# Gate rows through a scratch row in memory in place of TensorE transposes, in a two-layer decoder trunk

## What is computed

```python
for layer in range(DEPTH):
    mod = cond @ ada_w[layer] + ada_b[layer]
    sh1, sc1, g1, sh2, sc2, g2 = jnp.split(mod[:, None, :], N_MOD, axis=-1)
    h = rms_norm(x) * (1.0 + sc1) + sh1
    # layer 0: even_mixer (attention A and B), layer 1: odd_mixer (attention C)
    x = x + g1 * y
    h = rms_norm(x) * (1.0 + sc2) + sh2
    x = x + g2 * swiglu(h, ffn_w_in[layer], ffn_w_out[layer])
return rms_norm(x, final_norm)
```

## Time and profile before

| | |
|---|---|
| median of 3 runs | 2246.99 us (2246.51 to 2250.19) |
| profiled execution | 2246.95 us, of it the span 2245.2 us |
| PE busy | 2155.9 us (96%) |
| weight loads of PE (PEld) busy | 1783.2 us (79%) |
| DVE busy | 1622.7 us (72%) |
| ACT busy | 973.1 us (43%) |
| DMA | 594.08 MB, mean 265 GB/s |

### The profile page before, as it was taken

How to read it: one execution, slowest core, us unless ns; L and a number is a source line. 1 busy time by engine, 2 the same in 40 slices (tenths; PEclk the granted TensorE clock), 3 DMA queues, 4 the chain that set the end, 5 groups by cost and what they waited for, 6 DMA issues and landing times.

```text
span 2245.2 us, 26214 instructions
## 1 busy us (share of the span) xinstructions
PE 2155.9 (96%) x9996; PEld 1783.2 (79%) x9996; DVE 1622.7 (72%) x1696; ACT 973.1 (43%) x1276; POOL 10.0 (0%) x22
## 2 busy tenths in 40 slices
PE   3789999989999999999999999989999999999998
PEld 2578887878888888888887888878888888888886
DVE  5988898987789988777667666586665554555446
ACT  4344444454443344434445444454443344433444
POOL 0000000000000000000000000000000000000000
PEclk9899999999999999999999999999999999999999
DMA  9977878859889999977755533357765555555543
GB/s 389 421 290 311 330 300 356 329 230 372 325 325 353 385 381 378 383 284 288 283 213 230 197 127 117 122 189 300 283 249 202 199 188 187 187 190 196 193 152 150
DMA packets 82446, 594.08 MB, mean 265 GB/s; under 512 B 9296, under 2 KB 9328, under 8 KB 10672
## 3 DMA queue, kind: packets, MB, share of 16 engines
q1 hardware_dynamic: 81072, 588.29, 68.2%
q0 software_dynamic: 1280, 4.51, 0.7%
HBM read 590.66 MB, written 2.10 MB: 264 GB/s over the span
## 4 chain that ended last, share of the span: by engine, by line
PE 83%; DVE 10%; DMA 3%; ACT 2%; DVEq 1%; issue 0%; SPq 0%; ACTq 0%
PE ps L1344 25%; PE ps L1346 25%; PE ps L1345 25%; DVE w_lo L800 3%; PE ps L1332 2%; DVE ada_raw L804 2%; DMA gate<-in_ada 2%; DMA raw<-in_ffn_out 1%; PE ps L1439 1%; DVE gate L804 1%; PE ps L1372 1%; ACT w_hi L478 1%; PE ps L1374 1%; PE ps L1373 1%; DVE xT_lo L919 0%; PE ps L1438 0%
## 5 line engine op out<-in xcount | busy, mean ns | idle before, releaser
L800 DVE TENSOR_TENSOR w_lo<-raw,w_hi 128x1024 fp32r<-128x1024 f32 x728 | 880.5, 1222 | 470.3 <-ACT w_hi L478 466.1
L478 ACT ACTIVATE w_hi<-raw 128x1024 fp32r<-128x1024 f32 x728 | 763.0, 1060 | 987.3 <-PE ps L1346 801.6
L1344 PE MATMUL ps<-w_hi,xT_hi 128*128 128x512 f32 x1940 | 769.4, 397 | 31.8 <-DVE xT_lo L1057 24.3
L1346 PE MATMUL ps<-w_hi,xT_lo 128*128 128x512 f32 x1940 | 760.3, 392 | 0.0
L1345 PE MATMUL ps<-w_lo,xT_hi 128*128 128x512 f32 x1940 | 759.5, 392 | 0.0
L1344 PEld LDWEIGHTS ps<-w_hi,xT_hi 128*128 128x128 f32 x1940 | 367.3, 189 | 112.6 <-DVE xT_lo L1057 26.6
L1346 PEld LDWEIGHTS ps<-w_hi,xT_lo 128*128 128x128 f32 x1940 | 366.7, 189 | 78.0
L1345 PEld LDWEIGHTS ps<-w_lo,xT_hi 128*128 128x128 f32 x1940 | 367.5, 189 | 74.2
L804 DVE SCALAR_TENSOR_TENSOR ada_raw<-ada_raw,cond 128x2048 f32<-128x2048 f32 x176 | 401.8, 2283 | 16.8 <-DMA ada_raw<-in_ada 15.7
L1344 PE MATMUL ps<-w_hi,hT_hi 128*128 128x512 f32 x896 | 352.6, 393 | 2.7 <-DVE work L1243 1.1
L1346 PE MATMUL ps<-w_hi,hT_lo 128*128 128x512 f32 x896 | 349.5, 390 | 0.0
(11 more groups left out here) (178 smaller groups left out, 952.7 us busy)
## 6 DMA issues: line engine op xcount, KB each, us to landing
ada_raw<-in_ada SPq DMA_DIRECT2D x176, 1024.0 KB, 6.6
raw<-in_ffn_in SPq DMA_DIRECT2D x176, 1024.0 KB, 4.9
raw<-in_ffn_out SPq DMA_DIRECT2D x88, 1024.0 KB, 5.2
raw<-in_ab_in SPq DMA_DIRECT2D x48, 1024.0 KB, 8.3
raw<-in_swa_in SPq DMA_DIRECT2D x20, 1024.0 KB, 4.8
raw<-in_ab_out SPq DMA_DIRECT2D x16, 1024.0 KB, 7.3
raw<-in_swa_out SPq DMA_DIRECT2D x16, 1024.0 KB, 4.8
spare<-in_ada SPq DMA_DIRECT2D x8, 1024.0 KB, 8.2
```

The lines of the kernel that those rows point to most:

```text
L478: nc.scalar.activation(w_hi[:, p % PAIRS, :, :], raw[:, t % RAW, 2 * (p % 2):2 * (p % 2) + 2, :], ACT.Copy).then_inc(hi_ready, 1)
L800: tt(w_lo[:, p % PAIRS, :, :], raw[:, (p // 2) % RAW, 2 * (p % 2):2 * (p % 2) + 2, :], w_hi[:, p % PAIRS, :, :].bitcast(F32), ALU.subtract ...
L1344: mm(out, hi[:, kt, tok], w_hi[:, q % PAIRS, k, :], start=(kt == 2 * ps0), stop=False)
L1346: last = mm(out, lo[:, kt, tok], w_hi[:, q % PAIRS, k, :], start=False, stop=(kt == 2 * ps1 - 1))
```

## The change

GpSimd makes the gate rows. For each of the four gates it waits for `mods_ready`, writes the vector from `mod` to a scratch row in memory (`gate_rows`, new), waits until that has landed, and loads the row back, broadcast to all partitions, into `gate`. The loads wait for what frees the tile: `o_done` 4 or 12, or the `evacuated` count at the end of the projection before. DVE only waits for the landing; PE's transposes and its waits for the copy go. The order in GpSimd's queue is as in the diff: the write of the third row stands ahead of the first C bias, the third load behind the last bias of C_OUT, the fourth row ahead of `final_norm`.

```diff
+    rows = nc.dram_tensor("gate_rows", (4, D), F32, kind="Internal").ap()
...
-        gate_spread = sem("gate_spread")
-        gate_copied = sem("gate_copied")
+        row_written = sem("gate_row_written")
+        row_landed = sem("gate_row_landed")
...
+            def gate_row(n, vec):
+
+                pool.wait_ge(mods_ready, GATES_AT[n])
+                pool.dma_start(rows[n].rearrange("(k p) -> p k", p=P), mod[:, vec // 6, vec % 6, :], allow_slow_non_contiguous=True).then_inc(row_written, 16)
+                pool.wait_ge(row_written, 16 * (n + 1))
+
+            def load_row(n):
+                pool.dma_start(gate[:, :], rows[n].partition_broadcast(P)).then_inc(row_landed, 16)
+
+            gate_row(0, G1[0])
+            pool.wait_ge(o_done, 4)
+            load_row(0)
+            gate_row(1, G2[0])
+            pool.wait_ge(evacuated, EVAC_CREDIT + FFN[0][0][0].block0)
+            load_row(1)
+            gate_row(2, G1[1])
             for c in range(5):
...
+            pool.wait_ge(o_done, 12)
+            load_row(2)
+            pool.wait_ge(evacuated, EVAC_CREDIT + FFN[1][0][0].block0)
+            gate_row(3, G2[1])
+            load_row(3)
             pool.wait_ge(evacuated, EVAC_CREDIT + FFN[1][0][1].block0)
...
             def gate_row(n):
 
-                dve.wait_ge(gate_spread, n + 1)
-                nc.vector.tensor_copy(gate[:, :], bank(4, 4)).then_inc(gate_copied, 1)
-                dve.drain()
+                dve.wait_ge(row_landed, 16 * (n + 1))
...
-            def spread_gate(n, vec):
-
-                pe.wait_ge(mods_ready, GATES_AT[n])
-                for c in range(KT):
-                    last = tr(ps[:, 4 * 512 + c * P:4 * 512 + (c + 1) * P],
-                              mod[:, vec // 6, vec % 6, c:c + 1].broadcast_to([P, P]))
-                last.then_inc(gate_spread, 1)
-
...
-                if n == 12:
-                    spread_gate(0, G1[0])
-                if n == 14:
-                    pe.wait_ge(gate_copied, 1)
...
-                            if s == 0 and p == fout.pairs - 1:
-                                spread_gate(1 + 2 * layer, G2[layer])
...
-                    pe.wait_ge(gate_copied, 2 + 2 * layer)
...
-                if n == 16:
-                    spread_gate(2, G1[1])
...
-            pe.wait_ge(gate_copied, 3)
```

## The result

| | before | changed |
|---|---|---|
| median | 2246.99 us | 2256.02 us (2254.27 to 2258.07, 5 runs) |
| ratio to before | | 1.0040, 95% interval 1.0029 to 1.0051 |
| span of the profiled execution | 2245.2 us | 2253.8 us |

The changed kernel is slower by 0.4%, about 9 us. The forecast was 2242.8 us, with a range of 2238.5 to 2264 us.

What follows compares the result with a forecast made beforehand. TensorE was taken to bound the kernel (83% of the chain), with VectorE or the weight supply on it at two gate rows; -2.37 + 1.6 - 1.75 - 1.75 = -4.2 us gave 2242.8 us, range 2238.5 to 2264.

Steps and rivals of the forecast that it cites:

- Place 0, the gain: First gate row, copy ending at 424.16 us: VectorE's removed copy sets the gain, 2.37 us, not 1.75 + 2.37.
- Place 0, the write: Write of the first row at 306 to 316 us: charged nothing, up to W kept for the range.
- W: How long a row's write keeps the DMA engines from the weights: taken as 4 us, between 0 and 26.
- The row that was set aside, sinks: Transfer of 128 pieces of 128 bytes, all reading the same bytes; in proportion 26 us a write, not taken.
- the estimate of 1.3 us for W: From the skill page's 10.5 ns a packet, 128 packets; would put the sum 2.7 us lower.
- Place 1: Second gate row, copy at 687.19 us, chain through the weight supply: -2.37 + 4 = +1.6 us.
- Place 2: Third gate row, copy at 1455.25 us, TensorE bound: removing 16 transposes gains 1.75 us.
- Place 3: Fourth gate row, copy at 1708.38 us, TensorE bound: gain 1.75 us; row may land as late as 1712.9.
- rival (b): Row comes late through GpSimd's serial steps though W is small: 2244 to 2250 us, chance 0.17.
- Is the row in time at place 1?: Second row lands at 687.7 us; VectorE may stand until 689.6 before the chain is later than before.
- Rival (c): Small pieces hold the engines as beside sinks; no gain from W = 8.2, 2265 to 2281 us at 26; chance 0.23.
- The general form 2247 - 8.2 + W: Whole kernel's time for any W, as long as the second row isn't later than 689.6 us.

Runs made afterwards that it cites:

- the sorted row: Kernel before with rows 0, 1, 3 (then only 0, 3) written in 64-byte pieces, loaded into spare, put in feature order by ScalarE: ratios 0.9993 and 0.9990.
- writes only: Kernel before, transposes and copies kept, plus the four writes in 4-byte pieces, whose rows nobody reads: 2259.06 us, ratio 1.0049.
- place 0 alone: Kernel before with only the first gate row through memory, in 4-byte pieces, the others made as before: 2251.39 us, ratio 1.0015.
- the other execution: The changed kernel, unaltered, run and profiled again on another occasion, against the kernel before: 2255.11 against 2247.64 us, ratio 1.0038.

## Why the prediction was wrong, step by step

**Place 0, the gain.** Forecast 2.37 us; measured 2.4 in each of the four profiles in which that row was moved as in the change, 2.2 with the sorted row. DVE did set it, not the sum of both engines. Right.

**Place 0, the write (charged with 0).** This step failed. Its reason was that PE has no gap at 306 and DMA is less than half used soon after the earlier trace rows. The write cost 3.8 and 6.6 us in the two profiles of the change, 4.4 with writes only, some 5.8 by the ratio of place 0 alone. The two loads behind the write landed 7.8 and 7.7 us late, the stock ran out, and the slack that follows came too late for it; written at 332, with half of the hole in time without a load, it still cost 5.8. Where it cost most, a part is PE at its lower clock behind its stand, a term that the prediction didn't have. The text kept "up to W" for the range, so the doubt was there, but the sum took the end that was cheapest.

**W.** Taken as 4 us, between 0 and 26; measured 8.4 us at place 1. (That is against 410 GB/s. In the same stretch of the kernel before 0.6 us of it are missing too.) The mechanism of the step, engines that serve pieces and weights in turn, puts half of the feeding time on the weights. GpSimd's part in the feeding is 1.17 us (a price in proportion to the 128 rows of a broadcast load was 8.6), so the base of the estimate was wrong, and so was the half: while the pieces go, the weights get next to nothing. The row that was set aside, sinks with 34 to 164 GB/s, had the right form, one address or few; only its price per piece, 26 us / 128 = 200 ns, was too high. 8.4 us over 128 pieces an engine is 66 ns. The objection to it was that these pieces go to different addresses. So they do, but to neighbouring ones, and with 4 bytes in each 256 the hole became a dip. (In rows 6 six slices lie between 34 and 164 GB/s, not seven, and nine with the return, not ten, lack the 670 KB; the 26 us stand.)
On the page "DMA: Bandwidth & Descriptors" of the Trainium skill, the section "Rules for kernel authors" has a strided last dimension as one descriptor per element and wants it contiguous. The runs agree: some 13 us to landing against 5.3. Its section "Specifications" has an engine reading, modifying and writing below 512 bytes; that alone doesn't order these runs, since pieces of 64 bytes and pieces of 4 bytes 256 bytes apart are below it too and cost nothing that the medians show. By the estimate of 1.3 us for W from the section "Bandwidth" the sum would have been further off still; 8.4 is six times that.

**Place 1.** Forecast -2.37 + W. With W = 8.4 this is +6.0; measured +5.8 in both, or +6.3 and +6.1 up to pair 240. Right in that a hole at this place goes to the end, and mis-sized in W. That the sum comes out to 0.2 us is in part luck: it has no term for the clock, and 1.7 of the 5.8 us are PE at its lower level behind its second stand (the step at that pair is 1.6 us in both executions). Without it 4.1 us are left of the 6.0, so the delay of the supply didn't arrive in full; where the rest was made up, nothing here shows.

**Place 2.** Forecast -1.75, measured 0 (0.0 in both executions of the change, ratio 0.9999 alone). This step failed too. It took "PE bound" for granted and didn't ask what is next in PE's stream behind the transposes. It is a wait for DVE's half of an output block, which the transposes had covered.

**Place 3.** Forecast -1.75; measured -1.8 alone and -1.4 and -1.1 in the change. The row was late, as rival (b) had it. DVE stood 4.82 us, and PE noticed 0.3 (0.7 in the other execution): it had fallen back by 10.0 us by then, which moves the limit of 1712.9 to 1722.9, and the update began at 1723.3.

**Is the row in time at place 1?** Forecast 687.7 with the limit at 689.6. Its load was issued only at 686.53, so it could not be. It cost little or nothing of its own (DVE stood 0 and 0.66 us for it), since the same hole had kept DVE.

**The sum.** -2.37 + 1.6 - 1.75 - 1.75 = -4.2 was forecast. Measured in the same terms: -2.4 (place 0) + 5.2 (write 0, the mean of 3.8 and 6.6) + 6.2 (place 1) + 0 - 1.3 = +7.7; the medians say +9.0 and +7.5. Of the difference of 11.9 us the write at 306 has 5.2, place 1 with its W has 4.6, place 2 has 1.75. Rival (c) said that at W = 8.2 the change gains nothing, and nearest to what happened was its mild end; with W = 8.4 alone it would have been right by its own rule. (Its +24 us for W = 26 puts the lateness of the row, 15.5, at place 1. By the rule that W lengthens the chain in full it would be 26 - 2.37 = 23.6 there, and 8 us more in all.) It is slower because two further terms failed in the same direction. The general form 2247 - 8.2 + W holds one W; the kernel pays it twice.

**What stays open.** By the profiles the writes alone cost 4.4 + 8.5 = 12.9 us, and less the 6 us that the change saves (2.4 + 2.2 + 1.4) that is 6.9, within its 6.3 to 9.2; but the 2.2 comes from the same two profiles, so this tests little. By the ratio they cost 0.49%, 11.0 us, and less 6 that is 5, where 0.38 and 0.40%, 8.5 and 9.0 us, were measured. The intervals (6.3 and 4.9 us wide) leave room for that, and nothing here settles it. It isn't settled either whether it is the shared block in memory, the order of addresses or the 8 KB that they all lie in that makes the pieces slow; no run varied the distance between 4 and 256 bytes, or the spread at one distance.

## What to carry to other kernels

Before small pieces are written beside a saturated stream of loads, compare the pause they may cause with the stock that the engines hold (here four pairs, some 11 us at 2.7 us a pair when it is full, of which 9.8 us were there at place 1), not with the average use of the DMA engines: slack that comes later doesn't feed an engine now, and idle time helps only as far as the pause doesn't outlast it. A wait of PE can cost more than its length: behind a stand of 2.66 us the lower clock took another 1.7. Behind every piece of work that is taken off the bounding engine, look at its next instruction: if that is a wait for something which depends on the work ahead of the gap, the gap stays. And keep what a partition holds together on its way to memory: 128 pieces of 64 bytes did for nothing what 2048 pieces of 4 bytes did for 9 us; but then the price of undoing the order (0.71 us for each update, 3.8 us for each row) has to find an engine that has it to spare.

## What the runs showed of the hardware

A write of 8 KB in 2048 pieces of 4 bytes, 64 to each 256 bytes of memory, took 11 to 16 us to land. It kept all loads at 0 to 109 GB/s for 9 us at place 1, and at 0 to 96 for 13 us at 332 us, where for the first 6 of them hardly any load was out; the loads of weights behind it landed 5.5 to 7.8 us late at places 0 and 332. With each piece 256 bytes from the next it took 8.7 us in the median, and in the dip the loads kept 109 to 369 GB/s. In pieces of 64 bytes it took 1.7 to 7.3 us (medians of the four profiles 3.1 to 5.3), without a trace in the ratios. GpSimd's own part was 1.17 us for 2048 pieces and 0.54 for 128. A DVE multiplication of 128x1024 float32 with one operand in PSUM took 1.22 us, and 1.93 when the other one was read with a stride of 64 bytes; a copy of 128x2048 by ScalarE from a source with that stride took 3.8 us. PE, after 2.66 us of standing, ran at its lower clock level from 700 to 702 us, 0.50 granted, and partly so in the 2 us on either side (0.78 and 0.87).
